# Reordering the top-k pieces, the queries and the gate exponentials in a 256-expert gather stage of a two-block fp32 layer

## The reference

```python
def block(xb):                                   # T = 128 tokens
    qh = (xb @ w_pq).reshape(T, P_HEADS, 2, P_KEY_DIM)
    s1 = jnp.einsum('thd,nd->thn', qh[:, :, 0], sub_keys1)
    s2 = jnp.einsum('thd,nd->thn', qh[:, :, 1], sub_keys2)
    v1, i1 = lax.top_k(s1, P_TOPK)               # P_TOPK = 16 of 128 keys
    v2, i2 = lax.top_k(s2, P_TOPK)
    cand_s = (v1[..., :, None] + v2[..., None, :]).reshape(T, P_HEADS, P_TOPK * P_TOPK)
    cand_i = (i1[..., :, None] * P_NKEYS + i2[..., None, :]).reshape(T, P_HEADS, P_TOPK * P_TOPK)
    top_s, pos = lax.top_k(cand_s, P_TOPK)
    eidx = jnp.take_along_axis(cand_i, pos, axis=-1)
    g = jax.nn.softmax(top_s, axis=-1)
    a = jax.nn.gelu(jnp.einsum('thkd,td->thk', expert_down[eidx], xb), approximate=False)
    return jnp.einsum('thk,thkd->td', g * a, expert_up[eidx])
```

## Time and profile before

| | |
|---|---|
| median of 3 runs | 1511.7 us (1508.75 to 1513.2) |
| profiled execution, its own time | 1511.7 us |
| its span, first to last instruction | 1509.9 us |
| PE / DVE / ACT / POOL busy, share of the span | 86% / 63% / 39% / 18% |
| expert stage, 289 to 950 us: PE / DVE / ACT / POOL busy | 519 / 475 / 176 / 268 of 661 us |
| expert stage: share of the 16 DMA engines, rate | 1.00, 414 GB/s |
| before it, 0 to 289 us: share of the DMA engines | 0.40 |
| behind it, 950 to 1509.9 us: share of the DMA engines | 0.43 |
| the chain that ended last | PE 57%, DMA 23%, DVE 9%, ACT 7%, issue 3% |

### The profile page before, as it was taken

One profiled execution on the slowest core, in us unless ns is written; L12 is line 12 of the kernel. 1 busy time (PEld: TensorE's weight loads), 2 busy tenths in 40 slices (PEclk: granted clock), 3 DMA queues, 4 the chain that ended last, 5 costly groups with the idle time before them and its releaser, 6 DMA issues.

```text
span 1509.9 us, 17083 instructions
## 1 busy us (share of the span) xinstructions
PE 1304.7 (86%) x6376; PEld 935.1 (62%) x6376; DVE 945.7 (63%) x1973; ACT 594.9 (39%) x1027; POOL 275.0 (18%) x281
## 2 busy tenths in 40 slices
PE   7988999287878888787978777699999999999998
PEld 7977787242424343332424222597699999899887
DVE  5656455587776868777777765563555456666445
ACT  4555353232322322232222221554345753555334
POOL 1000000243433434343434332000000000000000
PEclk9998999699999999999999999899999999999999
DMA  7442252499999999999999999354243345455552
GB/s 265 152 148 95 95 189 89 158 422 422 421 421 415 410 421 401 421 420 421 391 421 421 421 421 410 132 196 139 84 168 115 137 151 184 150 193 173 201 191 76
DMA packets 56984, 398.82 MB, mean 264 GB/s; under 512 B 7096, under 2 KB 7352, under 8 KB 9032
## 3 DMA queue, kind: packets, MB, share of 16 engines
q0 software_dynamic: 36864, 268.45, 43.0%
q1 hardware_dynamic: 17856, 125.84, 23.8%
q10 hardware_dynamic: 2184, 3.45, 0.7%
HBM read 396.67 MB, written 1.05 MB: 263 GB/s over the span
## 4 chain that ended last, share of the span: by engine, by line
PE 57%; DMA 23%; DVE 9%; ACT 7%; issue 3%; POOL 1%; ACTq 0%; SPq 0%; DVEq 0%; POOLq 0%
PE ps L750 42%; DMA B<-in_ex,eidx 22%; PE ps L993 9%; DVE B L2043 3%; ACT hl L1232 2%; DVE hl L1717 2%; POOL B L714 1%; ACT diags L1472 1%; ACT L1467 1%; ACT L1454 1%; ACT av_ L1467 1%; DMA ring<-in_wt 0%; PE ps L1087 0%; PE ps L953 0%; PE ps L1054 0%
## 5 line engine op out<-in xcount | busy, mean ns | idle before, releaser
L993 PE MATMUL ps<-B,diags 128*128 128x512 f32 x1024 | 475.7, 609 | 153.9 <-ACT diags L1472 153.9
L993 PEld LDWEIGHTS ps<-B,diags 128*128 128x128 f32 x1024 | 187.0, 192 | 432.4 <-ACT diags L1472 243.1
L1717 DVE TENSOR_TENSOR hl<-ring,hl 128x2048 fp32r<-128x2048 f32 x118 | 270.1, 2291 | 269.9 <-ACT hl L1232 269.8
L714 POOL DMA_INDIRECT B<-in_ex,eidx x256 | 267.8, 1046 | 656.8 <-PE ps L993 363.4
L2043 DVE CUSTOM_DVE_ANT_0 B<-B 128x1024 f32<-128x1024 f32 x256 | 310.2, 1220 | 111.8 <-DMA B<-in_ex,eidx 111.4
L750 PE MATMUL ps<-XT,hl 128*128 128x256 f32 x2520 | 323.1, 291 | 8.2 <-DVE XT L1726 8.2
L750 PEld LDWEIGHTS ps<-XT,hl 128*128 128x128 f32 x2520 | 315.8, 198 | 14.2 <-DVE XT L1726 8.0
L1232 ACT ACTIVATE hl<-ring 128x2048 fp32r<-128x2048 f32 x118 | 224.7, 1907 | 126.0 <-PE ps L750 124.2
L1467 ACT ACTIVATE av_<-av_ 128x2 f32<-128x2 f32 x128 | 26.0, 203 | 431.8 <-DVE av_ L2043 431.7
L750 PE MATMUL ps<-hl,R 128*128 128x512 f32 x792 | 182.6, 391 | 0.0
L750 PEld LDWEIGHTS ps<-hl,R 128*128 128x128 f32 x792 | 147.9, 188 | 31.3 <-issue 0.8
(11 more groups left out here) (320 smaller groups left out, 918.4 us busy)
## 6 DMA issues: line engine op xcount, KB each, us to landing
ring<-in_wt SPq DMA_DIRECT2D x117, 1024.0 KB, 4.9
B<-in_ex,eidx POOLq DMA_INDIRECT x256, 13.0
X<-in_x SPq DMA_DIRECT2D x2, 512.0 KB, 4.1
B<-in_mem ACTq DMA_DIRECT2D x1, 1024.0 KB, 9.8
ring<-in_wple SPq DMA_DIRECT2D x1, 1024.0 KB, 5.0
out<-B SPq DMA_DIRECT2D x4, 256.0 KB, 2.0
GB<-in_gffn ACTq DMA_DIRECT2D x1, 512.0 KB, 3.7
GB<-in_gfin ACTq DMA_DIRECT2D x1, 512.0 KB, 3.5
```

Source lines behind the costliest of these rows:

```text
L714: e.indirect_dma_start(out=rows[i % NG][:, :], out_offset=None, in_=A["ex"], in_offset=bass.IndirectOffsetOnAxis(ap=eidx[:, tb, s:s + 1], ...
L993: m = e.matmul(acc[tb][hf][:, :], diags[:, i % 4, :], rows[i % NG][:, 1024 + 512 * hf:1536 + 512 * hf], start=(s == 0), stop=(s == 127))
L1717: e.tensor_tensor(w[1][:, :], ring[:, i % RING, :], w[0][:, :].bitcast(F32), ALU.subtract).then_inc(lo.sem)
```

## The change

Three things change. On ACT, `gates_exp(0, 0)` stands before the wait for XG and the load of gfin; `queries(h + 1)` goes from slot 2 to slot 1, `scores(h + 1)` from slot 4 to slot 3, and the other `gates_exp` from slot 2 to slot 5. On DVE, `gsub` goes behind the copy of the indices. And the stream that was 13 pieces ahead is no more: each group has the top-k of the next one, five pieces a slot, so that pieces 26 to 30, with `idx` as 28, `gsub` as 29 and the reciprocal as 30, fall in slot 5, and the last in slot 6. The split of DVE goes from slot 3 to slot 1. The top-k of group (0, 0) stands before XG. PE, POOL and SP are unchanged.

```diff
--- before.py
+++ after.py
@@ -1456,9 +1456,9 @@
             queries(0)
             e.wait_ge(*inv["h2"])
             scores(0)
+            gates_exp(0, 0)
             e.wait_ge(*xgs[0])
             fetch("gfin", GB[:, :], A["gfin"].partition_broadcast(128))
-            gates_exp(0, 0)
             for h in range(8):
                 for tb in range(2):
                     for n in range(8):
@@ -1471,11 +1471,11 @@
                                 e.wait_ge(*pe["ex", i + z - 4])
                             e.activation(diags[:, (i + z) % 4, :], ident[:, :], ACT.Copy,
                                          scale=av_[:, tb, s + z:s + z + 1]).then_inc(dgx.sem)
-                        if tb == 0 and h < 7 and n == 2:
+                        if tb == 0 and h < 7 and n == 1:
                             queries(h + 1)
-                        if tb == 0 and h < 7 and n == 4:
+                        if tb == 0 and h < 7 and n == 3:
                             scores(h + 1)
-                        if n == 2 and (h, tb) != (7, 1):
+                        if n == 5 and (h, tb) != (7, 1):
                             gates_exp(h + tb, 1 - tb)
 
 
@@ -1981,9 +1981,6 @@
                 e.wait_ge(*s)
                 s = yield from top16(cand, cand2, ts, pos)
                 e.wait_ge(*s)
-                gj = gw[:, tb, 16 * h:16 * h + 16]
-                e.tensor_scalar(gj, ts, ts[:, 0:1], None, ALU.subtract).then_inc(gsub.sem)
-                yield
                 e.tensor_scalar(pi[:, 0, :], pos[:, :], 4, None, ALU.logical_shift_right)
                 yield
                 s = step(e.tensor_scalar(pi[:, 1, :], pos[:, :], 15, None, ALU.bitwise_and))
@@ -2009,6 +2006,9 @@
                 e.wait_ge(*s)
                 e.tensor_copy(eidx[:, tb, 16 * h:16 * h + 16], ei).then_inc(idx.sem)
                 yield
+                gj = gw[:, tb, 16 * h:16 * h + 16]
+                e.tensor_scalar(gj, ts, ts[:, 0:1], None, ALU.subtract).then_inc(gsub.sem)
+                yield
                 e.wait_ge(*gexp[h, tb])
                 s = step(e.reciprocal(smx[:, 1:2], smx[:, 0:1]))
                 yield
@@ -2016,24 +2016,17 @@
                 ready[h, tb] = step(e.tensor_scalar(gj, gj, smx[:, 1:2], None, ALU.mult))
                 yield
 
+            for _ in topk(0, 0):
+                pass
             e.wait_ge(*at["gffn"])
             for tb in range(2):
                 m = e.scalar_tensor_tensor(XG[:, tb, :], X[:, tb, :], norm["h2"][0][:, tb:tb + 1], GB[:, :], ALU.mult,
                                            ALU.mult)
             m.then_inc(xgs.sem)
             e.wait_ge(*xgs[0])
-            for _ in topk(0, 0):
-                pass
-
-            def rest():
-
-                for g in range(1, 16):
-                    yield from topk(g // 2, g % 2)
-
-
-            ahead = rest()
             for h in range(8):
                 for tb in range(2):
+                    nxt = topk(h + tb, 1 - tb) if (h, tb) != (7, 1) else iter(())
                     e.wait_ge(*ready[h, tb])
                     for n in range(8):
                         i, s = 32 * h + 16 * tb + 2 * n, 16 * h + 2 * n
@@ -2046,11 +2039,12 @@
                         e.wait_ge(*gelu[i // 2])
                         e.tensor_tensor(av_[:, tb, s:s + 2], av_[:, tb, s:s + 2], gw[:, tb, s:s + 2],
                                         ALU.mult).then_inc(coef.sem)
-                        ops = ((4, 4, 4, 4, 2, 5, 4, 4) if h + tb else (8, 7, 7, 7, 2, 5, 4, 4))[n]
-                        for _ in range(ops):
-                            next(ahead, None)
-                        if tb == 0 and h < 7 and n == 3:
+                        for _ in range(5):
+                            next(nxt, None)
+                        if tb == 0 and h < 7 and n == 1:
                             split_to(min(32 + h, NUM["gq", 0, 0] - 1))
+                    for _ in nxt:
+                        pass
 
 
             for tb in range(2):
```

## The result

The changed kernel takes 1528.9 us (median of 4 runs, 1525.7 to 1532.9) against 1512.0 for the kernel before: a ratio of 1.0119, 95% interval 1.010 to 1.014, about 17 us. The forecast was 1538.7, in a range of 1518 to 1547, with 0.85 for slower. The direction and the place were right; the size came out at two thirds.

The account below looks back on a forecast made before the run. The DMA engines, full in the expert stretch, bound the kernel. Losses of 21.5 (h = 2 to 6), 1.8 (h = 1), 1.7 (start) and 3.2 (h = 0) made 28.2, 27 with a 5.8 us lead: 1511.7 + 27 = 1538.7, range 1518 to 1547.

Parts of the forecast that it names:

- G16: Gather of position 0 of the next group; forecast 5.5 us later than today, released by idx, 4.3 us too late.
- h = 2 to 6: 5 x 4.3 = 21.5 us: Expert stretch, heads 2 to 6: DMA engines idle 4.3 us once in each head, 21.5 us in all.
- third rival: Faster: a shorter way from query to next group's first gather wins back 7 us lost against the beat; 1505, chance 0.05.
- The lead of 6.0 us: Time from a gather's issue to its use with an empty queue, from the first gather; sets the next group's issue deadline.
- fifth rival: A shorter lead, 4.7 us, behind a queue just run dry: each head loses 1.1 less, 1531; chance 0.16.
- Gathers 12 to 15 ... have 2 us or more left: Last four gathers before the next group's first come 1.6 us later, with 2 us or more to spare.
- 1.7 us forecast for the start: Before the first rows: XG beside POOL's first issues costs 0.6, gfin's later 0.5 MB load 1.2; together 1.7 us.
- In tb = 1 nothing is lost: Groups with tb = 1 have no query; next group's first gather has 3.1 us to spare, so no loss.
- behind idx the wait for the Exp holds up nothing that counts: DVE's wait for the Exp behind idx holds up only slots 6 and 7, whose rows have landed.
- Halfway: Next group's first gather waits only for PE with p = 8, 0.9 us late for five heads; 1518, chance 0.12.
- No change: The queue covers the delay, or ACT's order binds nothing; 1511.7 to 1514, chance 0.10.
- the fourth: Worse than the sum: PE's clock falls in the new pauses, 1.7 us in each of seven heads; 1551, chance 0.10.

Follow-up runs that it names:

- e1: Changed kernel with ACT's queries and scores back in slots 2 and 4 and DVE's split back in slot 3: 1512.0 us, ratio 1.0005 to the kernel before.
- e2: Changed kernel with only ACT's scores moved back from slot 3 to slot 4: 1518.3 us, ratio 1.0059 to the kernel before.
- e11: Changed kernel with only ACT's queries back in slot 2, and DVE's split in slot 3: 1515.9 us, ratio 1.0036 to the kernel before.
- e3: Changed kernel with top-k pieces as 7, 7, 7, 7, 1, 0, 2, 0, so idx is ready in slot 3: 1522.6 us, ratio 1.0072 to before.
- e7: Kernel before with only ACT's order changed, queries in slot 1 and scores in slot 3: 1519.2 us, ratio 1.0045 to the kernel before.
- e8: Kernel before with the gates' Exp in ACT's slot 1 (first group excepted) and DVE's split in slot 2: 1509.0 us, ratio 0.9990.
- e10: Changed kernel with ACT's queries and scores in slots 2 and 4, DVE's split in slot 2, idx ready in slot 3: 1513.4 us, ratio 1.0022 to before.
- e6: Kernel before with only the new start, topk(0, 0) ahead of XG and first Exp ahead of gfin's load: 1511.0 us, ratio 1.0012.
- e5: Changed kernel with DVE's split back in slot 3: 1532.0 us, ratio 1.0161 to the kernel before.
- e4: Changed kernel with pieces as 5, 5, 5, 5, 5, 4, 2, 0, so DVE asks for the Exp in slot 6: 1537.3 us, ratio 1.0169 to before.
- e9: Changed kernel with DVE's wait for the Exp in slot 6 and an unused one-input sum on DVE in slot 5: 1531.7 us, ratio 1.0128 to before.

## Why the prediction was right, and where its size was off

**Direction, place, mechanism: shown.** The DMA engines run dry once in a head with a query, around G16; ACT's two waits and idx in slot 5 form one chain; taking ACT's waits out alone returns everything (e1), either wait alone a part (e2, e11), an early idx a part (e3), and ACT's order alone costs in the kernel before too (e7).

**The chain to G16: right within 8%.** From ACT's copy, forecast and measured in h = 1 (us after it): Gelu of slot 2 at 0.6 and 0.5; of slot 3 at 5.2 and 5.0; of slot 4 at 11.8 and 11.2; of slot 5 at 16.8 and 16.1; G16 at 18.9 and 17.5. Half of the miss is POOL's answer: from the Gelu of slot 5 to G16 I had 2.1 us, with the answer of the very first gather, and it is 1.4 (418.53 to 419.94), POOL starting 0.44 after the idx copy does.

**The term that was mis-sized: "h = 2 to 6: 5 x 4.3 = 21.5 us".** From G16 of h = 1 to G16 of h = 6 the kernel after takes 838.03 - 419.94 = 418.1 us, the kernel before 405.5: 12.6 more, 2.5 a head. The row of h = 6 in the kernel after:

```profile
838.03 0.94 POOL L714 DMA_INDIRECT B<-in_ex,eidx  x1 [6.45 <-DVE eidx L2007]
```

The first cause is the chain. G16 came 1.3 us sooner than forecast, in every head, which leaves 3.0 of the 4.3, and 2.8 after the 0.2 that the prediction takes off. What the DMA engines lost is about that. In the 8 us from 2 ahead of G16 they moved, in head 4 of the kernel after and then of the kernel before:

```profile
669.44:677.44 8.00, 5.26 (x12) 2.12 (x12) 5.89 (x17) 4.67 (x10) 3.79 (x4) 1.00 0.78 285
```
```profile
653.93:661.93 8.00, 7.79 (x19) 3.17 (x18) 7.29 (x25) 2.00 (x7) 4.34 (x4) 1.00 1.01 415
```

Against 421 GB/s, which most slices of this stage have in the profile of the kernel before, 285 is a loss of 2.6 us. Reckoned so, the kernel after loses 2.6 to 3.0 us in each of heads 2 to 6, 1.7 in head 0 (forecast 3.2) and 1.2 in head 1 (forecast 1.8), 17.0 in all.

The second cause: the whole of it was booked as loss against the kernel before, as if that lost nothing there. It loses 3.1 us in the same seven stretches, 1.3 of them in head 3 and 1.0 in head 5. These belong to the 7 us by which it misses the ideal beat, which stood in my third rival. Against this, the kernel after fills up slowly: in the 19 us behind each of the stretches it moves 405 to 419 GB/s, the kernel before 410 to 424, which is 2.3 us more in seven heads. An estimate with all three is 27 - 7 x 1.3 - 3.1 + 2.3 = 17.1 us, and 17 was measured.

e1, whose G16 is early enough, takes (819.12 - 415.43) / 5 = 80.7 us a head, the kernel before 81.1 and the kernel after 83.6. e8 and e10 say that an earlier G16 wins back at most 2 of the 7 us. The row of e1 for its h = 6:

```profile
819.12 0.94 POOL L714 DMA_INDIRECT B<-in_ex,eidx  x1 [2.93 <-DVE eidx L2007]
```

**The lead of 6.0 us.** It puts the deadline 14.5 us behind the copy. The stage loses nothing at 13.1 and 13.3, 2 us at 14.7 (e11) and 17 at 17.5, so it is about right, with e2's and e7's late gathers as the reservation. The kernel after also shows the lead itself. Of G16 in head 4, with one gather still under way, the view of line 714 says:

```profile
DMA to landing us min/median/max: 5.5/5.5/5.5
```

In heads 2 to 6 it is 5.3 to 5.8 us from issue to landing, and 5.5 for that kernel's first gather. So the fifth rival (a lead of 4.7, 1531) fell on its mechanism, although its time is nearer to the 1528.9 than my 1538.7 is. The estimate of 4.5 us that the prediction works out from the Trainium skill ("DMA: Bandwidth & Descriptors", section "Latency and other measured facts") is too short for this gather as well, and that its 1529 is the measured time is luck: it goes with a G16 at 18.9. With G16 at 17.5 that lead would leave 1.5 us a head, and e2 with 15.4 would have lost nothing instead of 7.

**"Gathers 12 to 15 ... have 2 us or more left": wrong for e7, by the rates above, and doubtful for the changed kernel**, whose engines move 360 to 403 GB/s in the 12 us ahead of G16 in heads 2 to 6; the kernel before has 417 to 421 there in three of these heads, but 370 and 352 in the two others.

**The start and the split.** 1.7 us forecast for the start; 1.2 in the stage of e6, its ratio not told from 1. The split on DVE is hidden behind ACT's wait, as forecast, in the profile of e5.

**"In tb = 1 nothing is lost", "behind idx the wait for the Exp holds up nothing that counts".** The first held: in all sixteen groups idx releases the gather, but the short stretches with a DMA share of half are those of tb = 0. The second held for the wait and missed what it protects (e4).

**Signs.** Of the signs that I named, two came out otherwise: the share in the 10 us behind G16 is 0.83 to 0.93, not below 0.8, as the gap is short; and in slot 0 of tb = 1 the first dot waits for no DMA, since DVE reaches it after G16 has landed, and the second waits 0.8 to 1.1 us. G16 came 23.4 us after the query's start, not 24.7. The others came as named.

**The rivals.** Halfway (idx does not bind) fell: eidx ends all sixteen waits. No change and faster fell with the time. Of the clock: the granted clock was 1.00 in the pauses (the windows above) and 0.98 over the stage as before, so the fourth fell as well. The fifth stands under the lead.

## What to carry to other kernels

When a stage is bound by a queue of transfers, don't ask which engine got slower but when the next transfer can be issued, and write down the chain to that issue across all engines; a function that waits for a matmul in ACT's program holds up every later Gelu, whoever needs it. Price a lateness against what the kernel before already loses at that place, not against an ideal beat. And an idle engine can be of use: see whether a wait that looks free keeps a two-input DVE instruction away from a DMA that POOL is just issuing.

## What the runs showed that was not expected

- POOL's issue of an indirect gather takes 0.94 us alone and 0.94 beside a one-input reduction of 1.64 us (e9). When it begins while a dot (128x1024, two inputs in SBUF, 1.22 us) is running, it ends 0.81 us after the dot, which makes 1.81 in e4. Taking away 1.5 us of idle time on DVE made the kernel 8 us slower.
- Between 10 and 13 us behind the query's copy, moving the next group's first gather brings nothing that the runs can tell from none; 4 us more cost 17 us over seven heads.
